# Feeding the first feed-forward stage unscaled x, with the RMS factor and the shift applied at the end of a unit

## The reference, cut to what matters

```python
ada = (silu(c) @ w_ada + b_ada)                  # 9 vectors of 2048 channels: shift, scale, gate for 3 sub-layers
n = rms_norm(x, g_ffn1) * (1 + scale) + shift    # x / sqrt(mean(x*x over channels) + eps)
hu = n @ w1_in                                   # 2048 -> 2 * 5632
h, u = split(hu)
x = x + 0.5 * gate * ((silu(h) * u) @ w1_out)    # 5632 -> 2048
```

## Time and profile before

| | us |
|---|---|
| median of three timed runs | 2592.71 |
| lowest and highest of them | 2592.57 and 3062.14 |
| the profiled execution: its time | 2591.88 |
| the profiled execution: span of its slowest core | 2590.2 |
| TensorE busy in the span | 2498.0 (96%) |
| VectorE, ScalarE, GpSimd busy | 1044.5, 436.0, 340.1 |

### The profile page before, as it was taken

The page is one execution under the profiler, slowest core; times in us unless marked ns, Lnnn a source line. Parts: engine busy times, 40 slices in busy tenths (PEclk is TensorE's granted clock), DMA queues, the critical chain, the costliest instruction groups (busy, mean ns, idle before and its releaser), DMA issues.

```text
span 2590.2 us, 38329 instructions; the slowest of 8 cores (2579.1 to 2590.2 us)
## 1 busy us (share of the span) xinstructions
PE 2498.0 (96%) x14726; PEld 1403.9 (54%) x14726; DVE 1044.5 (40%) x1553; ACT 436.0 (17%) x784; POOL 340.1 (13%) x609
## 2 busy tenths in 40 slices
PE   1999999999999999999999999999999999999997
PEld 0666666666666666677544444444444444444445
DVE  5468555555555436647732224610121101111026
ACT  3513100010000013523511111510000000000013
POOL 1221111111111110000111100000000000000034
PEclk9999999999999999999999999999999999999998
DMA  9998998999998974843385552454444444444445
GB/s 222 146 161 160 225 172 146 172 170 171 170 171 144 167 137 92 193 83 63 77 182 86 86 106 41 82 98 81 71 83 75 74 74 82 77 71 80 68 63 167
DMA packets 104465, 310.06 MB, mean 120 GB/s; under 512 B 11872, under 2 KB 27232, under 8 KB 104160
## 3 DMA queue, kind: packets, MB, share of 16 engines
q0 software_dynamic: 79600, 260.12, 61.3%
q1 hardware_dynamic: 24688, 47.50, 5.6%
HBM read 546.09 MB, written 16.78 MB: 217 GB/s over the span
## 4 chain that ended last, share of the span: by engine, by line
PE 90%; DMA 4%; DVE 3%; ACT 1%; issue 1%; SPq 0%; DVEq 0%; POOL 0%; ACTq 0%; POOLq 0%
PE ps L278 90%; DMA ring<-w_head 2%; DMA hT<-xT 1%; ACT nT L288 1%; DVE U L292 1%; DVE hT L292 1%; DVE rs L309 1%; DMA U<-hT 0%; SPq L611 0%; DVE hT L303 0%; ACT L288 0%; ACT rs L288 0%; DVE rs L292 0%; SPq L340 0%; DVEq L1115 0%
## 5 line engine op out<-in xcount | busy, mean ns | idle before, releaser
L278 PE MATMUL ps<-nT,ring 128*128 128x352 bf16 (+3 forms) x9344 | 1650.0, 339 | 14.5 <-DMA ring<-w_head 6.7
L278 PEld LDWEIGHTS ps<-nT,ring 128*128 128x128 bf16 x9344 | 913.4, 98 | 737.4 <-issue 22.5
L278 PE MATMUL ps<-U,ring 128*128 128x352 bf16 (+3 forms) x4480 | 793.3, 339 | 1.9 <-DMA U<-hT 1.8
L278 PEld LDWEIGHTS ps<-U,ring 128*128 128x128 bf16 x4480 | 435.3, 98 | 353.7 <-issue 4.0
L288 ACT ACTIVATE tmp<-ps 128x512 f32<-128x512 f32 (+1 forms) x262 | 139.9, 536 | 1680.3 <-PE ps L278 1658.5
L292 DVE TENSOR_TENSOR U<-tmp,ps 128x352 bf16<-128x352 f32 (+1 forms) x184 | 110.1, 600 | 747.3 <-PE ps L278 737.3
L303 DVE SCALAR_TENSOR_TENSOR hT<-ps,ghT,hT 128x352 f32<-128x352 f32 (+3 forms) x288 | 182.7, 635 | 347.7 <-PE ps L278 347.6
L325 POOL DMA_DIRECT2D ring<-w_in x208 | 110.8, 533 | 1230.7 <-PE ps L278 1216.1
L388 DVE SCALAR_TENSOR_TENSOR ring<-ring,rs 128x2048 bf16<-128x2048 bf16 x112 | 253.3, 2285 | 4.8 <-DMA ring<-w_adaD 4.7
L325 POOL DMA_DIRECT2D ring<-w_out x118 | 63.1, 535 | 522.5 <-PE ps L278 513.6
L303 DVE SCALAR_TENSOR_TENSOR tmp<-ps,pp_sb,tmp 128x512 f32<-128x512 f32 x54 | 40.6, 751 | 172.6 <-ACT tmp L288 156.1
(11 more groups left out here) (67 smaller groups left out, 603.7 us busy)
## 6 DMA issues: line engine op xcount, KB each, us to landing
ring<-w_in POOLq DMA_DIRECT2D x208, 512.0 KB, 6.4
ring<-w_adaD POOLq DMA_DIRECT2D x112, 512.0 KB, 13.2
ring<-w_out POOLq DMA_DIRECT2D x80, 512.0 KB, 6.4
hT<-xT SPq DMA_DIRECT2D x8, 2112.0 KB, 23.3
ring<-w_ada POOLq DMA_DIRECT2D x32, 512.0 KB, 16.2
ring<-w_out POOLq DMA_DIRECT2D x38, 384.0 KB, 5.7
hscr<-hT SPq DMA_DIRECT2D x16, 512.0 KB, 13.5
hT<-hscr SPq DMA_DIRECT2D x16, 512.0 KB, 12.1
```

Of the source, the lines that this page charges most:

```text
L278: e.matmul(o, l, r, start=st, stop=sp, skip_group_check=sk),
```

## The change

- x is loaded by chunk into four staging chunks of `hT` (12 to 15); the next load of a staging chunk follows the modulation of the one in it. The first fill waits for nothing.
- ScalarE applies gs to unscaled x. The shift of the chunk is written as column 1,056 of `nT` (`TW` = 1,088 wide), and the third block of each piece is 353 columns wide, so that it also gives w . shift; that column is gathered in `bcol`.
- The squares are summed in `rs` as the chunks come; the square roots follow items 29 and 31.
- A unit's end (`finish`) multiplies h by r on GpSimd, applies Silu with the bias on ScalarE, multiplies u by r on VectorE, and closes with (u + bias) * silu on VectorE. It is queued and run eight units later: three ends in each of the last pieces of units 8 to 11, seven in each of units 12 to 15.
- Units 12 to 15 (`raw_unit`) do the same straight from PSUM, and they have one tick each instead of three; `nT` gets its scaled and shifted content (`rms_apply`) in the first out phase. Units 16 to 31 have three ticks each, units 32 on two or three.
- Pieces: unit 0 4, 4, 4, 4; units 1 to 7 3, 4, 4, 5; units 8 to 11 three pieces, 6, 6, 4 (44 pieces instead of 48). `HEAD_ORDER` is another one. x is read again by 16 DMAs, each after the end of the unit that was parked there.

```diff
@@ first fill, loads of x
-                first_rd = [Bh.r(11)] if not slot_used else []
...
-        for g4 in range(4):
-            S.add("sp", lambda e, g4=g4: e.dma_start(
-                out=hT[:, g4 * 4:(g4 + 1) * 4, :],
...
+        def x_load(kc):
+            S.add("sp", lambda e: e.dma_start(out=hT[:, stage(kc), :], in_=xtv[:, kc, :]),
+                  writes=[Bh.r(stage(kc))], dma=("x", kc % NST))
+        for kc in range(NST):
+            x_load(kc)
@@ order
+    "a0 a1 a2 a3 a4 a5 u1.0 u3.0 u5.0 u4.0 a6 a7 u6.0 a8 "
+    "a9 u0.0 a10 u2.0 u7.0 a11 a12 u8.0 a13 u11.0 a14 u1.1 u10.0 u2.1 "
+    "u6.1 a15 a16 u9.0 a17 u5.1 a18 u4.1 u3.1 a19 a20 u7.1 a21 u0.1 "
+    "u7.2 u3.2 u4.2 u1.2 a22 a23 u5.2 u6.2 u9.1 u2.2 a24 u10.1 u0.2 a25 "
+    "u8.1 a26 a27 a28 a29 u11.1 a30 a31 u0.3 u1.3 u2.3 u3.3 u4.3 u5.3 "
+    "u6.3 u7.3 u8.2 u9.2 u10.2 u11.2 "
@@ ffn
                     if q > q_first:
                         tick()
-                        tick()
-                        if q0 == 0 or q % 2 == 0 or q % 8 in (1, 7) and q0 == 16:
+                        if q0 > 0:
                             tick()
-                    ffn_evict(q - q0, pair_mm(sh, su, tbs, False), tbs)
+                        if q0 == 16 or q0 == 32 and q % 3:
+                            tick()
+                    if s == 0 and q0 == 0:
+                        raw_unit(q, sh, su)
+                    else:
+                        ffn_evict(q - q0, pair_mm(sh, su, tbs, False), tbs)
...
+                if s == 0 and q0 == 0:
+                    run_late(0)
+                    rms_apply(0, 0, 0, T)
                 if q1 < NH:
                     for d in range(KC):
                         tick()
+                        if s == 0 and q0 == 0 and d + 1 < KC:
+                            rms_apply(0, d + 1, 0, T)
@@ head
-            def x_scale(kc):
-                op_tt(hT[:, kc, :], hT[:, kc, :], rs[:], ALU.mult, [Bh.r(kc), Brs.r(0)], [Bh.r(kc)])
+            def x_square(kc):
+                o, r = (rs[:], Brs.r(0)) if kc == 0 else (tmpflat[:, 0:T], Btmp.rr(0, 3))
+                op_act(o, hT[:, stage(kc), :], AF.Square, [Bh.r(stage(kc))], [r])
+                if kc:
+                    op_tt(rs[:], rs[:], tmpflat[:, 0:T], ALU.add, ...)
             def x_mod(kc):
-                op_act(nT[:, kc, :], hT[:, kc, :], AF.Identity, ... bias=adaT[:, kc:kc + 1], scale=gsT[:, kc:kc + 1])
+                op_act(nT[:, kc, 0:T], hT[:, stage(kc), :], AF.Identity, ... scale=gsT[:, kc:kc + 1])
+                op_copy(nT[:, kc, T:T + 1], adaT[:, kc:kc + 1], ...)
+            def finish(u, x, y):
...
+                op_tt(h, h, rs[:, x:y], ALU.mult, [hr, Brs.r(0, x, y)], [hr], eng="pool")
+                op_act(tmp[:, ti, 0:w], h, AF.Silu, ..., bias=bias_ap(u, 0))
+                op_tt(g, g, rs[:, x:y], ALU.mult, [gr, Brs.r(0, x, y)], [gr])
+                def close():
+                    op_stt(Bp.ap3[:, u, x:y], g, bias_ap(u, 1), tmp[:, ti, 0:w], ALU.add, ALU.mult, ...)
+                    if y == T and u >= 6:
+                        x_reload(2 * (u - 6))
+                        x_reload(2 * (u - 6) + 1)
+                return close
...
                     if i % 2 == 1:
...
+                        if kc + 2 < KC:
+                            x_square(kc + 2)
+                        x_mod(kc)
+                        if kc + NST < KC:
+                            x_load(kc + NST)
+                        if kc >= KC - 2:
+                            roots = TB3[0:2] if kc == KC - 2 else TB3[2:3]
+                            for (x, y) in roots:
+                                x_root(x, y)
...
+                        if y == T:
+                            bias_col(u, hu, bk, w, "act" if p == 0 else False)
+                if last:
+                    fins += [(u, x, y) for (x, y) in TB3]
+                    if u >= 8:
+                        emit_finish()   # three times
@@ units 12 to 15
+        def raw_unit(q, sh, su):
+            bks = pair_mm(sh, su, RAW_BLKS, False)      # (704, T + 1), (0, 352), (352, 704)
...
+                op_tt(tmp[:, t1, 0:w], psum[bh][:, 0:w], rs[:, x:y], ALU.mult, ...)
+                op_act(tmp[:, t1, 0:w], tmp[:, t1, 0:w], AF.Silu, ..., bias=bias_ap(q, 0))
+                op_tt(tmp[:, t2, 0:w], psum[bu][:, 0:w], rs[:, x:y], ALU.mult, ...)
...
+                run_late(0)
+                late.append(close)                      # op_stt into Bp, as in finish
+                for f in more_fins * (3 if x == 704 else 2):
+                    f()
```

More of the change, by code:

```diff
@@ L905, in head_fill, with bias_r @@
             return fill_slot([(w1_head[u][:, 2 * P * k0:2 * P * k1], 1, 2 * P * n, 0)])
-        def ffn1_head():
[L908 to L911, removed]
-            def x_scale(kc):
-                op_tt(hT[:, kc, :], hT[:, kc, :], rs[:], ALU.mult, [Bh.r(kc), Brs.r(0)], [Bh.r(kc)])
-            def x_mod(kc):
[L917 to L923, removed]
-                    writes=[Bh.rr(c0, c1)], dma=("xr", key))
-            for kc in range(4):
-                x_scale(kc)
+        def bias_r(u, hu):
+            return Bbc.r(0, 2 * u + hu, 2 * u + hu + 1)
@@ new lines, in bias_ap, with bias_col @@
+        def bias_ap(u, hu):
+            return bcol[:, 2 * u + hu:2 * u + hu + 1]
+        def bias_col(u, hu, bk, w, first):
+            if first == "act":
+                op_act(bias_ap(u, hu), psum[bk][:, w:w + 1], AF.Copy, [psr(bk)], [bias_r(u, hu)])
+            elif first:
+                op_copy(bias_ap(u, hu), psum[bk][:, w:w + 1], [psr(bk)], [bias_r(u, hu)])
+            else:
+                op_tt(bias_ap(u, hu), bias_ap(u, hu), psum[bk][:, w:w + 1], ALU.add, [psr(bk), bias_r(u, hu)], [bias_r(u, hu)])
@@ L941, in ffn1_head @@
                 n = k1 - k0
-                last = len(KCUTS[u]) - 1
-                pk = [park(u, hu) for hu in range(2)]
+                last = p == len(KCUTS[u]) - 1
                 for (x, y) in TB3:
                     w = y - x
-                    ti = tctr[0] % 4
+                    wx = w + 1 if y == T else w
                     for hu in range(2):
@@ L962, in ffn1_head @@
-                    if p == last:
-                        def fin(u=u, x=x, y=y, w=w, ti=ti, pa=pa, pr=pr):
-                            op_tt(Bp.ap3[:, u, x:y], tmp[:, ti, 0:w], pa, ALU.mult, [Btmp.r(ti, 0, w), pr], [Bp.r(u, x, y)])
-                        late.append(fin)
-                        run_late(1)
-            run_late(0)
-            nbanks[0] = 8
-            cb = Btn.ap3.rearrange("p a b -> p (a b)")[:, 0:D]
-            S.add("sp", lambda e: e.dma_start(out=cb, in_=cbc), writes=[Btn.rr(0, 2)], dma="cb")
@@ L971, in ffn1_head @@
-            for i in range(0, KC, 4):
-                x_reload(i, i + 4, i)
+                        if y == T:
[4 more added lines that the diff above has]
+                        emit_finish()
+                        emit_finish()
+                        emit_finish()
+            nbanks[0] = 8
+            cbuf = hT[:, KC - 4:KC - 2, :].rearrange("p a b -> p (a b)")[:, 0:D]
@@ L974, in make_sbc @@
+            S.add("sp", lambda e: e.dma_start(out=cbuf, in_=cbc), writes=[Bh.rr(KC - 4, KC - 2)], dma="cb")
+            x_reload(KC - 2)
+            x_reload(KC - 1)
+            more_fins.append(emit_finish)
             def make_sbc():
-                op_act(sbc, cb, AF.Silu, [Btn.rr(0, 2)], [SBC_R])
+                op_act(sbc, cbuf, AF.Silu, [Bh.rr(KC - 4, KC - 2)], [SBC_R])
+                x_reload(KC - 4)
+                x_reload(KC - 3)
             tickq.append(make_sbc)
@@ L990, in ffn1_head, with close @@
             return NHEAD
+        more_fins = []
+        RAW_BLKS = [(704, T + 1), (0, 352), (352, 704)]
+        def raw_unit(q, sh, su):
+            bks = pair_mm(sh, su, RAW_BLKS, False)
+            for (bh, bu), (x, y) in zip(bks, RAW_BLKS):
+                if y > T:
+                    y = T
+                    for hu, bk in enumerate((bh, bu)):
+                        bias_col(q, hu, bk, y - x, True)
+                w = y - x
+                t1, t2 = tctr[0] % 4, (tctr[0] + 1) % 4
+                tctr[0] += 2
+                op_tt(tmp[:, t1, 0:w], psum[bh][:, 0:w], rs[:, x:y], ALU.mult, [psr(bh), Brs.r(0, x, y)], [Btmp.r(t1, 0, w)])
+                op_act(tmp[:, t1, 0:w], tmp[:, t1, 0:w], AF.Silu, [Btmp.r(t1, 0, w), bias_r(q, 0)], [Btmp.r(t1, 0, w)],
+                       bias=bias_ap(q, 0))
+                op_tt(tmp[:, t2, 0:w], psum[bu][:, 0:w], rs[:, x:y], ALU.mult, [psr(bu), Brs.r(0, x, y)], [Btmp.r(t2, 0, w)])
+                def close(q=q, x=x, y=y, w=w, t1=t1, t2=t2):
+                    op_stt(Bp.ap3[:, q, x:y], tmp[:, t2, 0:w], bias_ap(q, 1), tmp[:, t1, 0:w], ALU.add, ALU.mult,
+                           [Btmp.r(t2, 0, w), bias_r(q, 1), Btmp.r(t1, 0, w)], [Bp.r(q, x, y)])
+                run_late(0)
+                late.append(close)
+                for f in more_fins * (3 if x == 704 else 2):
```

(2 more changed lines are left out.)

87 lines of the change are left out of this document (57 added, 30 removed), and 6 rows, old and new, of the table HEAD_ORDER.

## The result

The changed kernel is slower: ratio of its runs to those of the kernel before 1.0068, 95% interval 1.0048 to 1.0088, which is 17.6 us (12 to 23). The profiled execution has a span of 2610.1 us, on core 2, against 2590.2 on core 4, the slowest cores of the two. (The comparison leaves out executions in which the clock of a whole die was lowered; medians that include them are not used.) The prediction said 2591, range 2578 to 2603; even the fastest run, 2609.42, lies outside.

What follows compares the result with a forecast made beforehand. TensorE was taken as the bound, except at the start, where DMA matters. 2591.88 - 7.8 (head) + 7.5 (units 16 to 31) + 0.5 (small) = 2592.1 us, stated as 2591, range 2578 to 2603.

Steps and rivals of the forecast that it cites:

- Term 1: Head, up to unit 12: DMA limits before the last conditioning item, TensorE behind it; 7.8 us less, bounds 2 to 13.
- Sum 196.5 us ... 200.0 ... u0.3 can start at 202.7 us: Head: DMA time for x, items and 137 pieces ahead of item 31, then landing, item and modulation, before the last stretch.
- Reloads come after the ends in units 13 to 15 ... No cost.: Loads of x on SP's queue: reloads come 28 us before first use and cost nothing.
- VectorE adds a lag of 2.3: Last pieces of units 8 to 11: VectorE falls behind, banks absorb most, TensorE waits 2.3 us in all; 0 to 6.
- 1.8 again: Last stretch of the head: 1.8 us lost to the 1.2 GHz level after the thin items, as before the change.
- rival (b): Last pieces and units 12 to 15: GpSimd and VectorE hold each other; 2600 us, up to 2605; chance 0.18.
- The hinge: Last conditioning item, item 31, in the head: before it DMA is the limit, behind it TensorE, with 330 matmuls instead of 402.
- Term 2: Units 16 to 31: five fills a unit make DMA fall back 1.33 us a unit; 7.5 us more, bounds 4 to 9.
- the out phase behind ... gives it back: Out phase after unit 31: asks only 2 fills in 7.2 us, so DMA's lag from units 16 to 31 is recovered there.
- (a): Units 16 to 31: no starving in the middle, the head's gain stays; 2584 us, down to 2578; chance 0.22.
- (c): Start of the head: chunks of x come late, each pair of items costs 2 us more; 2605 to 2615; chance 0.05.
- (d): Head: larger pieces bring weights to 167 GB/s, 12 us more gained; 2580 us, or 2572 without VectorE's lag; chance 0.05.

Runs made afterwards that it cites:

- e2: Changed kernel with the load of c and the reloads queued behind it held until unit 11's last piece is in; ratio 1.0051 to the kernel before.
- e12: Changed kernel with the twelve late ends of units 0 to 3 replaced by two ScalarE copies each (result not the reference's); one execution, 2614.27 us.
- e3: Changed kernel without GpSimd's 36 products of h by r (factor missing in units 0 to 11); ratio 1.0063 to the kernel before.
- e6: Changed kernel with the late ends spread: one each after units 6 and 7, two after 8 to 10, three after 11; ratio 1.0060 to the kernel before.
- e11: Changed kernel with spread ends, late load of c, earlier ticks, reciprocals after last modulation, GpSimd's products before fills in units 12 to 15; ratio 1.0011 to kernel before.

## Why the prediction was wrong

**Term 1 (head, -7.8 us; measured +6.4 by unit 16 on average).** Three steps failed.

*"Sum 196.5 us ... 200.0 ... u0.3 can start at 202.7 us", set against the time measured before.* The same sum for the kernel before, 4.5 + 25.8 + 161.1 (125 pieces) + 3.5 + 0.5, gives 195.4, and its cores measure 199.4: the sum was 4 us early, and only one side of the difference was a sum. The difference itself, 5.1 us of bytes more ahead of item 31, was nearly right: 6.3 measured. Since item 31's end differs by core from 193.0 to 204.4 us in one execution of the kernel before, one core's row was no calibration for it either: 263.87 us is core 4's start of unit 12, and the mean is 261.4.

*"Reloads come after the ends in units 13 to 15 ... No cost."* The load of c and two reloads wait for no end; SP issued them from 197 to 212 us, 2.1 MB next to the fills of the last item and pieces. e2: 3.5 us at the begin of the stretch, 2.3 by unit 16. I followed what waits for a unit's end, and not what is left in the queue that waits for nothing.

*"VectorE adds a lag of 2.3", clock "1.8 again".* From the stretch's begin to unit 16 it lasts 9.8 us over the matmuls' price, where 4.1 were expected. e12 puts 8.3 us down to the ends of units 0 to 3, e3 puts 2.6 of them down to holding. The operation prices held: in e3, with nothing held, VectorE takes 5.5 us for a unit's last piece and ends (forecast 5.6). What failed is the lag made of them: without any hold TensorE waits 4.2 us for VectorE, not 2.3, and why the banks gave less room than forecast stays open. The holds came on top; they are rival (b), whose mechanism is now seen and whose price was too high: it let each of 36 products stretch one or two operations, 8 us in sum, and the trace has three operations held on a core, 3.7 us, of which 2.6 reach the time. Rows 13 showed the mechanism, and it should have been in the sum. That each wait also brought a piece at the lower clock (granted 0.91 from 260 to 280 us) was left out for waits on VectorE.

Together: unit 12 was forecast at 256.1 us and starts at 267.9 on average, 6.2 us of it from the later begin of the stretch and 5.6 from the stretch itself; the mean of the kernel before lies 2.5 us ahead of the row that was taken. That makes the 14.2 us between -7.8 and +6.4.

The hinge as a mechanism stood: DMA ahead of item 31, TensorE behind it, 72 matmuls fewer behind it worth 10.7 us. +9.0 at the begin of the stretch, -10.7 for the matmuls, +8.2 for the excess (9.8 against 1.5) make +6.5, against +6.4 read directly.

**Term 2 (middle, +7.5; measured +11.0, and 1.3 in the out phase).** The mechanism was right, and so was its size up to unit 31: w_in and the slower matmuls cost 7.5 us. What lies above it is the out phase, 3.5 us before it and 1.3 in it. Landings of a unit's first fill in the changed kernel, at 456, 499, 542, 571 and 647 us:

```profile
ring<-w_in POOLq DMA_DIRECT2D x1, 512.0 KB, 6.8
...
ring<-w_in POOLq DMA_DIRECT2D x1, 512.0 KB, 10.8
...
ring<-w_in POOLq DMA_DIRECT2D x1, 512.0 KB, 14.1
...
ring<-w_in POOLq DMA_DIRECT2D x1, 512.0 KB, 17.5
...
ring<-w_in POOLq DMA_DIRECT2D x1, 512.0 KB, 19.2
```

6.8 (for unit 18) to 17.5 (for unit 26) is 1.34 us a unit, as forecast (1.33). The first wait comes in unit 25, where 26 was forecast, by a hair: its fill takes 16.4 us with 16.2 to spare. The step that failed is "the out phase behind ... gives it back": the first w_out tile is issued in the same row as a unit's fills and has no more slack than they have; issued at 666.16 us, it is due 14.6 us later and lands after 18.8. TensorE waits 4.36 us for it (3.5 on average), and the clock is lower around that wait (granted 0.96 from 660 to 700 us, 116.02 us for the 768 matmuls of the out phase in place of 114.72).

**Rivals.** (a), no starving, fell. (b) held in kind, at a third of its price. (c), late chunks of x, fell: the 16 loads land in 10.4 us (median), and TensorE waits 60.6 us for fills and 2.2 for modulations. (d), a higher rate, fell: 26.5 MB of weights by 200 us, against 26.4 before. Of the signs named beforehand for a wrong forecast, the first one came: a last stretch waiting for VectorE.

**The sum.** With the terms as measured: -10.7 + 9.0 + 8.2 + 11.0 + 1.3 - 1.4 = +17.4 us. Two terms of opposite sign had been made to cancel; both were too favourable, and the range, built around the cancelled sum, was too narrow on the slow side: its parts' own upper bounds (head -2, middle +9, lag 6 instead of 2.3) gave 2603 to 2604 at most, and 4 us of systematic error and a queue not followed were in none of them.

## What to carry to other kernels

An earlier start is worth nothing where DMA was already full from the start to a later hinge, as here: count the bytes ahead of the hinge in both versions, and take the difference against a sum that reproduces the measured time of the version at hand. List every load that a change leaves without a wait, and see where it goes out. A ring that is level at 4.75 fills a unit can run out at 5; the first tile of the next stage belongs to the stage that runs out.

## What the runs showed of the hardware

- A VectorE operation with two SBUF inputs is held by GpSimd's products. In the changed kernel and in e6 it is held until the whole row ends, past products that began after it: 3.02 us in place of 0.52 beside a row of four, 3.04 beside five, each ending 0.4 us after the row. In e11 the engines can also take turns: an operation of VectorE ends at 257.76 us between two products of GpSimd, which take 1.13 and 1.20 us instead of 0.93, so that both lose. What decides between the two is not shown. Adds with a PSUM input took their 0.52 us beside the same rows. The Trainium skill, "GPSIMD Engine Reference", section Specifications, says that the SBUF interfaces are shared and contended for by VectorE's instructions with two SBUF inputs; these traces agree in both, and e3, without GpSimd's products, has none of these operations over its 0.52 to 0.58 us.
- Eight cores with the same work end item 31 up to 11 us apart (193.0 to 204.4 us before, 200.1 to 209.5 after): the cores get their bytes at different rates. In the changed kernel core 0, the earliest, had moved 36.8 MB by 200 us, and core 4, among the latest, 35.3.
- The queue lets landings grow unseen: with ten slots ahead, the fills of the new head take 23 to 33 us to land in the median of each size (16 to 21 before), and TensorE may still be just in time.
